# Layer 0's heads with turned copies first, the gate's reciprocal in halves, closing products with the last head last, and a store in eight blocks

## The reference

```python
def even_mixer(hc, hl, w_in, gate_b, head_g, qk_g, sink, rope, need_ctx):
    aq_l, ak_l, av_l, ao_l, ag_l, bq_l, bk_l, bv_l = split_cols(hl @ w_in, EVEN_SPLITS)
    ...
    h_ctx, h_lat = mlstm_bidirectional(...)            # 4 heads of 128, both directions
    ...
    b_lat = window_attention(group(q_l, B_KV), k_l, heads(bv_l, B_KV), k_c, v_c, sink)
    lat = jnp.concatenate([mlstm_out(h_lat, ao_l, head_g, hl.dtype), b_lat], axis=-1)
    ...

def mlstm_out(h, o, head_g, dtype):
    h = rms_norm(jnp.swapaxes(h, 1, 2), head_g.reshape(A_HEADS, A_DIM))
    return (jax.nn.sigmoid(o.astype(f32)) * h.reshape(h.shape[:2] + (A_WIDTH,))).astype(dtype)

# in first_block, per layer
x_lat = x_lat + mod_l[2] * (mix_l @ w_out[l])
```

## Time and profile before

| | us |
|---|---|
| median of 3 runs | 1713.38 |
| lowest and highest run | 1712.33, 1714.7 |
| the profiled execution's own time | 1714.8 |
| its span | 1713.5 |
| TensorE busy | 1613.1 (94% of the span) |
| VectorE busy | 1063.3 (62%) |
| ScalarE busy | 668.5 (39%) |
| granted TensorE clock, mean | 0.982 |

### The profile page before, as it was taken

How to read it: one execution, slowest core, us unless ns; L and a number is a source line. 1 busy time by engine, 2 the same in 40 slices (tenths; PEclk the granted TensorE clock), 3 DMA queues, 4 the chain that set the end, 5 groups by cost and what they waited for, 6 DMA issues and landing times.

```text
span 1713.5 us, 24182 instructions
## 1 busy us (share of the span) xinstructions
PE 1613.1 (94%) x9260; PEld 1306.6 (76%) x9260; DVE 1063.3 (62%) x1985; ACT 668.5 (39%) x1261; POOL 409.8 (24%) x345
## 2 busy tenths in 40 slices
PE   7999999889999999989888999989999999989888
PEld 5555565448888888866666999988888888779677
DVE  4567878458777788747767788555544555133821
ACT  1432433133333332344442555544444444134411
POOL 1012102001111110115430111026555554013401
PEclk9899999999999999999999999999999999999999
DMA  9323223223343466502325455544443333325131
GB/s 350 128 99 115 89 68 136 98 73 131 141 142 143 145 210 208 195 21 99 113 85 199 156 186 177 192 151 149 135 136 124 123 130 129 129 95 181 50 129 37
DMA packets 63827, 231.18 MB, mean 135 GB/s; under 512 B 7408, under 2 KB 8432, under 8 KB 63456
## 3 DMA queue, kind: packets, MB, share of 16 engines
q1 hardware_dynamic: 60800, 218.65, 37.4%
q0 software_dynamic: 2192, 6.29, 1.1%
q10 hardware_dynamic: 720, 4.68, 0.7%
HBM read 228.55 MB, written 1.05 MB: 134 GB/s over the span
## 4 chain that ended last, share of the span: by engine, by line
PE 88%; DVE 7%; ACT 3%; issue 2%; POOL 1%; DMA 0%; DVEq 0%; ACTq 0%; POOLq 0%
PE ps L240 15%; PE ps L258 11%; PE ps L260 11%; PE ps L259 11%; PE ps L1218 4%; PE ps L1219 3%; PE ps L1220 3%; PE ps L1845 3%; PE ps L725 2%; PE ps L248 2%; PE ps L715 2%; PE ps L618 2%; PE ps L387 2%; PE ps L302 1%; PE ps L1660 1%
## 5 line engine op out<-in xcount | busy, mean ns | idle before, releaser
L273 DVE TENSOR_TENSOR weights_rest<-ring,weights_rounded 128x1024 fp32r<-128x1024 f32 x181 | 246.0, 1362 | 63.6 <-ACT weights_rounded L267 63.5
L267 ACT ACTIVATE weights_rounded<-ring 128x1024 fp32r<-128x1024 f32 x207 | 216.6, 1053 | 96.1 <-PE ps L1220 94.1
L258 PE MATMUL ps<-h_hi,weights_rounded 128*128 128x512 f32 (+1 forms) x640 | 215.0, 336 | 0.0
L259 PE MATMUL ps<-h_lo,weights_rounded 128*128 128x512 f32 (+1 forms) x640 | 215.0, 336 | 0.0
L260 PE MATMUL ps<-h_hi,weights_rest 128*128 128x512 f32 (+1 forms) x640 | 215.0, 336 | 0.0
L1204 POOL TENSOR_TENSOR big<-scratch 128x512 f32<-128x512 f32 (+1 forms) x44 | 64.2, 1460 | 410.2 <-DVE scratch L1190 410.2
L1144 ACT ACTIVATE scratch<-ps,vectors 128x512 f32<-128x512 f32 (+1 forms) x88 | 59.2, 672 | 191.2 <-PE ps L260 182.1
L240 PE MATMUL ps<-h,ring 128*128 128x512 f32 x288 | 131.4, 613 | 2.2 <-DVE h L471 2.2
L240 PE MATMUL ps<-mix,ring 128*128 128x256 f32 (+1 forms) x448 | 126.4, 444 | 5.2 <-DVE mix L967 4.7
L259 PEld LDWEIGHTS ps<-h_lo,weights_rounded 128*128 128x128 f32 x640 | 121.5, 190 | 12.6
L258 PEld LDWEIGHTS ps<-h_hi,weights_rounded 128*128 128x128 f32 x640 | 121.5, 190 | 12.6
(11 more groups left out here) (324 smaller groups left out, 3636.5 us busy)
## 6 DMA issues: line engine op xcount, KB each, us to landing
ring<-in_up SPq DMA_DIRECT2D x88, 512.0 KB, 3.9
ring<-in_ada_rest SPq DMA_DIRECT2D x80, 512.0 KB, 4.4
ring<-in_a_in SPq DMA_DIRECT2D x80, 512.0 KB, 3.5
ring<-in_down SPq DMA_DIRECT2D x44, 512.0 KB, 3.5
ring<-in_even SPq DMA_DIRECT2D x20, 512.0 KB, 3.5
ring<-in_ada_first SPq DMA_DIRECT2D x16, 512.0 KB, 8.2
ring<-in_wout SPq DMA_DIRECT2D x16, 512.0 KB, 3.5
ring<-in_odd SPq DMA_DIRECT2D x16, 512.0 KB, 3.5
```

Of the source, the lines that this page charges most:

```text
L258: te.matmul(bank[:, 0:n], wh[:, k, :], hi(k), start=k == 0, stop=False)
L259: te.matmul(bank[:, 0:n], wh[:, k, :], lo(k), start=False, stop=False)
L267: sc.activation(pair[0], place(*key), ACT.Copy).then_inc(*mark("rounded", *key))
L273: ve.tensor_tensor(pair[1], place(*key), pair[0].bitcast(F32), ALU.subtract).then_inc(*mark("rest", *key))
```

## The change

It has four parts.

1. In layer 0's rounds, VectorE's copies 0 and 2 move ahead of the context part's probabilities. ScalarE's copy 3 moves between the four squares and the rest of the head's norm.
2. On VectorE the "+1" and the reciprocal of the gate move ahead of the attention's copy into `mix`. The reciprocal is cut into two instructions of 256 columns, with copy 4 between them.
3. The first of the eight closing products waits for the pieces of `mix` one by one. In layer 0 it takes the blocks in the order 0, 1, 2, 4, 5, 6, 7, 3, starts after the third head (`mixed_heads`, 2), waits for the fourth round's attention ahead of block 7 and for the fourth head ahead of block 3. In layer 1 the order stays 0 to 7, with waits ahead of blocks 0, 4 and 7. The other seven products are as before.
4. SP stores each of x's eight blocks (128 KB) as soon as it is closed, and waits for all of them at the end.

```diff
--- before.py
+++ after.py
@@ -226,8 +226,8 @@
             sp.dma_start(RING[:, p * D:(p + 1) * D], d[arr][index, :, :]).then_inc(ev.sem(f"weights_in_{p}"), 16)
         for k in range(KD):
             sp.wait_ge(*at("closed", 1, k))
-        sp.dma_start(out, xv[:, :, LAT]).then_inc(*mark("stored", step=16))
-        sp.wait_ge(*at("stored"))
+            sp.dma_start(out[:, k, :], xk(k)).then_inc(*mark("stored", k, step=16))
+        sp.wait_ge(*at("stored", KD - 1))
 
 
 
@@ -726,11 +726,9 @@
                                         PT[(g + o) % len(PT)][:, p:p + cols], start=first, stop=last)
                 ins.then_inc(*mark("weighed", key, g // 2))
 
-    def weigh_copies(eng, odd, key, groups, tbanks, PT, pt_free=(), between=None):
+    def weigh_copies(eng, odd, key, groups, tbanks, PT, pt_free=(), only=None):
         for j, group in enumerate(groups):
-            if between and j == len(groups) // 2:
-                between()
-            if j % 2 != odd:
+            if j % 2 != odd or (only and j not in only):
                 continue
             eng.wait_ge(*at("turned", key, j))
             if j >= len(PT):
@@ -891,13 +889,15 @@
             sc.activation(v3(dn[:, 4 * t:4 * t + 2], 1), v3(BANK[NUM[t]], 256)[:, :, 128:129],
                           ACT.Abs).then_inc(*mark("denominators", i, t))
 
-        def head_norm():
+        def head_squares():
             for t in range(4):
                 sc.wait_ge(*at("heads", i, t))
                 if t:
                     sc.wait_ge(*at("head_square", i, t - 1))
                 sc.activation(qa, hs[:, 128 * t:128 * t + 128], ACT.Square,
                               accum_out=dn[:, 4 * t + 2:4 * t + 3]).then_inc(*mark("head_square", i, t))
+
+        def head_norm():
             ss, rr = v3(dn, 4)[:, :, 2:3], v3(dn, 4)[:, :, 3:4]
             sc.wait_ge(*at("head_square", i, 3))
             sc.activation(ss, ss, ACT.Ln, bias=EPS[:, 0:1], scale=1.0 / AD).then_inc(*mark("head_log", i))
@@ -909,7 +909,11 @@
                 ins = sc.activation(h, h, ACT.Copy, scale=dn[:, 4 * t + 3:4 * t + 4])
             ins.then_inc(*mark("heads_normed", i))
 
-        weigh_copies(sc, 1, E, groups0(i), TB0, PT0, between=head_norm)
+        weigh_copies(sc, 1, E, groups0(i), TB0, PT0, only=(1,))
+        head_squares()
+        weigh_copies(sc, 1, E, groups0(i), TB0, PT0, only=(3,))
+        head_norm()
+        weigh_copies(sc, 1, E, groups0(i), TB0, PT0, only=(5,))
 
     def dve_even(i):
         us, E = units0(i), ("even", i)
@@ -955,13 +959,15 @@
             ve.wait_ge(*at("forward_head", i, t))
             ve.scalar_tensor_tensor(h, b[:, 256:384], dn[:, 4 * t + 1:4 * t + 2], h, ALU.mult,
                                     ALU.add).then_inc(*mark("heads", i, t))
+        weigh_copies(ve, 0, E, groups0(i), TB0, PT0, only=(0, 2))
         dve_probs(us[1])
-        weigh_copies(ve, 0, E, groups0(i), TB0, PT0)
+        ve.tensor_scalar(sg0, sg0, 1.0, None, ALU.add).then_inc(*mark("sigmoid_sum", "even", i))
+        ve.wait_ge(*at("sigmoid_sum", "even", i))
+        ve.reciprocal(sg0[:, 0:CTX], sg0[:, 0:CTX])
+        weigh_copies(ve, 0, E, groups0(i), TB0, PT0, only=(4,))
+        ve.reciprocal(sg0[:, CTX:TOK], sg0[:, CTX:TOK]).then_inc(*mark("sigmoid", "even", i))
         ve.wait_ge(*weighed(E, groups0(i)))
         ve.tensor_copy(MIX[:, (4 + i) * TOK:(5 + i) * TOK], BANK[3]).then_inc(*mark("mixed_attention", i))
-        ve.tensor_scalar(sg0, sg0, 1.0, None, ALU.add).then_inc(*mark("sigmoid_sum", "even", i))
-        ve.wait_ge(*at("sigmoid_sum", "even", i))
-        ve.reciprocal(sg0, sg0).then_inc(*mark("sigmoid", "even", i))
         ve.wait_ge(*at("sigmoid", "even", i))
         ve.wait_ge(*at("heads_turned", i))
         ve.scalar_tensor_tensor(MIX[:, i * TOK:(i + 1) * TOK], BANK[5], v(V_HG + i), sg0, ALU.mult,
@@ -985,8 +991,17 @@
 
     def pe_wout(layer):
         n = TOK if layer == 0 else SEQ
-        te.wait_ge(*(at("mixed_heads", AH - 1) if layer == 0 else at("mixed_near", 3)))
-        for b in range(KD):
+        order, waits = ((0, 1, 2, 4, 5, 6, 7, 3), {0: at("mixed_heads", AH - 2), 7: at("mixed_attention", AH - 1), 3: at(
+            "mixed_heads", AH - 1)}) if layer == 0 else ((0, 1, 2, 3, 4, 5, 6, 7), {0: at("mixed_global", 3),
+                                                         4: at("mixed_near", 2), 7: at("mixed_near", 3)})
+        w = v3(place("wout", layer, 0), 128)
+        te.wait_ge(*loaded("wout", layer, 0))
+        for x, k in enumerate(order):
+            if k in waits:
+                te.wait_ge(*waits[k])
+            ins = te.matmul(BANK[0][:, 0:n], w[:, k, :], mixk(n)(k), start=x == 0, stop=x == KD - 1)
+        ins.then_inc(*mark("product", "wout", layer, 0))
+        for b in range(1, KD):
             if b >= 4:
                 te.wait_ge(*at("residual", layer, b - 4))
             pe_product(("wout", layer, b), BANK[b % 4], n, mixk(n))
```

## The result

| | before | changed |
|---|---|---|
| median of 5 runs, us | 1713.38 | 1704.77 |
| lowest and highest, us | 1712.33, 1716.11 | 1702.28, 1705.02 |
| the profiled execution's own time, us | 1714.8 | 1703.43 |
| its span, us | 1713.5 | 1702.1 |
| granted TensorE clock, mean | 0.982 | 0.985 |

The ratio is 0.9946, with a 95% interval of 0.9935 to 0.9957: 9.2 us faster, 7.4 to 11.1 (the two medians lie 8.6 us apart). The forecast was 1704.0 us.

The account below looks back on a forecast made before the run. TensorE, busy 94% of the span, was taken as the bound. Terms of -10.1 us took the profiled 1714.8 to 1704.7, and half of its 1.4 us over the median gave 1704.0; 8-in-10 range 1700.5 to 1708.7.

Parts of the forecast that it names:

- The bound: Whole kernel: TensorE is busy 94% of the span, so edits on other engines count only where TensorE waits for them.
- The round's end: Layer 0's rounds: the 2.01 us hole is broken up, copy 4 comes later; 0.26 us longer, three times, +0.8 us.
- The closing products: End of layer 0: TensorE no longer waits 4.71 us for the last piece of `mix`; -4.4 us.
- The clock: Third round and closing products: both falls to 1.2 GHz behind long idle stretches go; -1.6 and -1.9 us.
- Rival A: Third round and closing products: the clock falls stay despite the broken-up holes; 1708.2 us, chance 0.17.
- Booking half of the 1.4 us: Profiled run 1.4 us over the median: half put to the third round's clock, already booked, moving 1704.7 to 1704.0.
- The sum: All booked terms: +0.8 - 4.4 - 1.6 - 1.9 - 0.5 - 2.5 = -10.1 us.
- Layer 1: Layer 1's closing products: the first starts without its 0.53 us wait; -0.5 us, bound 0.
- the store: Program end: the last store, 128 KB, lands in 2.3 us instead of 4.8; -2.5 us, bounds -1.3 and -2.6.
- B: Rounds' gate reciprocal: half costs as much as the whole, copy 4 1.6 us later still; 1711.1 us, chance 0.08.
- C: Rounds: copy 4 behind the reciprocal starves TensorE and the clock falls every round; +2.7 us, 1717.5, chance 0.03.
- D: Behind layer 0: an earlier start saves more, as low clock stretches fall on idle time; up to 3 us, 1701, chance 0.11.

Follow-up runs that it names:

- store alone: The kernel before with the final store in eight blocks and nothing else: 1711.13 us against 1712.46, ratio 0.9992.
- closing product alone: The kernel before with only each layer's first closing product in the new order with its waits cut up: 1705.93 us, ratio 0.9959.
- closing product and store: The changed kernel without its edits to the rounds (copies, probabilities, reciprocal and head norm as before): 1704.36 us, ratio 0.9949.
- the experiment with the whole one: The changed kernel with the whole reciprocal of 512 columns ahead of copy 4: 1712.52 us, ratio 0.9994.

## Why the prediction was right

**The bound.** TensorE's holes at these places were what counted: of the 4.71 us ahead of the closing products 4.5 came off between the two profiles. VectorE's own savings in rounds one to three brought nothing, as forecast.

**The round's end.** The sequence came as worked out: copies first, then turns held by the probabilities, then copy 4 behind half a reciprocal. The half took 1.75 us, as taken between 1.68 and 3.35. Of the forecast pieces of idle time, 0.7, 0.4 and 1.1 us, the first came as 0.88, the second lies within the turns (eight instructions took 1.42 us, 1.10 before), and the third as 0.93. In the frame of the kernel before (2.45 us added) the weighing of 2 and 3 began at 301.12 and the last one at 303.14, where 301.1 and 303.13 were forecast. What I had too short are the weighings themselves: 1.08 us for the one and 1.01 for the other, not 0.95 and 0.94. So the hole is 0.93 us, not 1.1, and a round got longer by 0.34 us where 0.26 was forecast: the term's sign, which is against the purpose of the edit, was right.

**The closing products.** -4.5 us for -4.4, and no wait for either piece of `mix`. What I had not seen is that this needs nothing of the edits to the rounds: with the late gate TensorE still comes 1.2 us after it.

**The clock.** Both falls were gone in the profile of the changed kernel, -3.3 us of -3.5 forecast. The term of the closing products was 0.2 us too large: the first addition stands 7.07 us behind the first matmul at full clock too, so the fall had cost 1.7 us and not 8.73 - 6.86 = 1.87. Rival A is refuted: behind the holes of 0.88 and 0.93 us there was no fall in any of the twelve rounds of three profiles. The second fall stands in both profiles that have the hole of 4.7 us (before, store alone). The first came and went: four profiles with the old rounds (before, store alone, closing product alone, closing product and store) show six falls in sixteen rounds. The Trainium skill's page "TensorE: Matmul & The Clock Gate" (What's actually happening) says that the gate follows recent activity on a beat that does not start with the kernel. The traces agree in so far as, with the same code in the rounds, the fall stood in round three before and in rounds one and two with the store alone. How many falls the median run of before had is on no record. Booking half of the 1.4 us for that was a choice that nothing supported; it moved the forecast by 0.7 us and did no harm.

**The sum.** The booked terms came to -10.3 us for -10.1. The other -1.1 us between the two profiles are low stretches of the clock outside the edited places, one fewer at the start and one in a dearer spot behind layer 1; by the medians the change is worth 8.6 us where 9.4 were forecast. That the forecast hit the median within 0.8 us is partly luck: runs of either kernel differ by more.

**Layer 1 and the store.** 0.6 us for 0.5. The store was the term off most: 2.95 us, outside the lower bound of 2.6 that I had drawn from a 64 KB load on another queue; a store of 128 KB from SP lands in 1.9 us. The Trainium skill's page "DMA: Bandwidth & Descriptors" (Anatomy of one DMA) fits about 2.0 us of fixed cost to transfers that GpSimd issues. This store, issued by SP, took less in all; for it the measurement decides.

**The rivals.** B and C rested on a reciprocal whose halves cost the whole; the experiment with the whole one shows that B's mechanism is real (1712.5 measured, 1711.1 by B's sum), and the halves of 1.75 us that its premise was false. D, more saved by low stretches elsewhere, came in the profile to 1.1 us and not in the median.

## What to carry to other kernels

Where several engines meet at the end of a round, list for each product the last input it waits for, and put nothing long ahead of it on the engine that makes it, however useful the long one is later: the reader of the gate's reciprocal stood behind at least 6 us of TensorE's work (seven blocks at 0.86 us), yet the change put half of the reciprocal ahead of a copy that TensorE was waiting for. A sum over blocks can start with what is ready and take the late block last, which made the hurry on the other engine unneeded. Split a final store so that the last transfer is small (5.63 us from the last block's closing to the end became 2.68).

## What the runs showed that was not expected

- A hole of 2.0 us cost a second time in 6 of 16 rounds, through the clock (1.6 us each), one of 2.5 us in 3 of 4, and holes of 0.9 us never (12 rounds). Breaking a hole up made the round 0.34 us longer and yet cost nothing in the median.
- Runs of one kernel differ with their mean clock: the kernel before by up to 6 us (0.36%) at 0.980 to 0.984, the changed kernel by up to 8 us at 0.982 to 0.988. A verdict on 1 to 3 us needs runs at the same clock, or the trace.
- VectorE's reciprocal goes by columns: 3.35 us for 512, 1.75 for 256, both on 128 partitions.
